# Half of modulation group 1 summed by TensorE with the pieces as weights, two first low parts ahead of the second sum, and later mLSTM numerators

## The chip, the cores and the metric

The kernel runs on one core of a Trainium2 chip. The metric is device time in microseconds (us) of one launch. TensorE (PE) does matrix products, VectorE (DVE) and ScalarE (ACT) elementwise work, GpSimd (POOL) masks and padding, and SyncE (SP) issues most of the transfers from the chip's memory.

## What is computed

Two transformer-like blocks follow each other on 256 positions of width 2048, batch 1, in float32. In both, a condition vector modulates the normalised input. Cut to what matters here:

```python
# first_block, for l in range(2)
c_act = silu(c)
mod = c_act @ ada_w[l] + ada_b[l]              # 2048 x 6144 weights
shift, scale, gate = split(mod, 3)
h = rms_norm(x, norm_g[l]) * (1.0 + scale) + shift
z = h @ w_in[l]
...
# second_block
mod = silu(c_2) @ w_ada_2[0] + b_ada_2[0]      # 2048 x 12288 weights, six parts
...
# bidirectional mLSTM, 4 heads of 256, d = forward, backward
num = sum over s of weight[t, s] * v[s]
den = sum over s of weight[t, s]
h_a = sum over d of num / max(|den|, exp(-m))
h_a = h_a * rsqrt(mean(h_a ** 2)) * g_head_a * sigmoid(oa)
mixed = concatenate([h_a, h_b]) @ w_out_2
```

## The kernel before

**Modulation.** The twelve parts (shift, scale, gate, ...) are twelve groups of 2048 columns. The 2048 rows of a group are read as 32 pieces (`AU`): in piece j each partition has 1024 values (`AC`) of one row, so that all of them are multiplied by one value of the condition, that of the partition in `c_act[:, 0, j]`. Partitions 0, 2, 4, ... carry one half of the columns and 1, 3, 5, ... the other (`CB2` is 2). DVE adds each piece, times its scalar, to an accumulator (`ada_start` for groups 0 and 1, `ada_add` for the others). When a group is complete, PE sums the accumulator over its partitions (`reduce_mod`): the accumulator's 128-column slices are the weights, and the moving operand has 128 columns, the last two of which are `halves_of`, one column for the even and one for the odd partitions. `mod_out` then adds the bias from PSUM into `mod`. Groups 0 and 1 (shift and scale of the first norm) must be complete before the first product of the kernel can start; groups 2 to 11 are added one piece per weight unit beside the products.

Groups 0 and 1 have an accumulator of twice the width (`ada_acc0`, `ada_acc1`), filled by turns, and a ring of eight slots (`FSLOTS`) of 512 KB, four in `ada_raw` and four in `ada_first`. SP (lines 549 to 552) issues the 64 pieces in order and, for each from the ninth on, first waits on `ada_used` until DVE has added the piece eight before. Behind them on SP's queue stand the units of the weight ring. From group 2 on the ring is the four slots of `ada_raw` (`ASLOTS`).

**Products.** Weights come in units of 512 KB (four 128-row tiles of 256 columns) into a ring of eight slots (`w_raw`). For most products ACT rounds a unit to its high part (`w_hi`, line 730), DVE subtracts (`w_lo`, line 1068), into rings of four slots (`PARTS`), and PE makes three matmuls per tile and half (high by high, low by high, high by low), all from line 1554. A block of 256 columns has four units over a contraction of 2048. Each engine walks the list `prods`; DVE and ACT prepare a block ahead (`ahead`, `prep`), and pieces of the modulation ride on the units (`ada_pieces`). The first product is `lat` of layer 0; its first four units are prepared by `prep(prods[0], 0, 0)`, which stands on DVE behind `mod_out(1)`.

**First norm.** `norm(0, ...)` on DVE computes `gainA` from `mod` group 1, then for each of 16 tiles the scaled tile (line 1108) and, two tiles later, its low part (line 1113); ACT makes the high part (line 773). With `by_tile`, the first block of `lat` takes the tiles one by one as they come ready.

**mLSTM.** It runs beside the product `out2b` (8 blocks of 2 units, 16 steps; nothing is split there), three steps to a head from step 3 on (`mlstm` on PE, ACT and DVE). In step 0 PE makes the head's scores into `bankS` and broadcasts the rows of direction 0 into `bankT`; in step 1 it broadcasts direction 1 and sums the squares of the head before (`head_sum`); in step 2 it makes, for each direction, the denominator into `stat` (`summed`) and the numerator into `bankO` (line 1828). `stat` and `bankO` each have one place: the second denominator waits until DVE has read the first (line 1430), the second numerator until DVE has read the first (line 1436). DVE's `head_output` divides both in step 0 of the next head. The last head's `head_output` and what follows it (`head_norm`, `head_low`) lead to `out2a`, a product with the mLSTM's output, 8 blocks of 2 units; PE's first block there waits unit by unit: the second unit needs all four heads.

Of the kernel before, what the change touches and what calls it, by code (L numbers as in the profile page):

```python
# [22 lines left out]
P = 128  # L23
T = 256
# [27 lines left out]
AC_T = AC // P  # L52
ASLOTS = 4
# [42 lines left out]
def program(nc, a, out):  # L96
# [3 lines left out]
    with ctx:  # L100
# [70 lines left out]
        c_raw = at("c_raw", W1 + 20, [P, 2, AU])  # L171
        W2 = W1 + 16 + CT * UW * 4 / 1024
# [72 lines left out]
        halves_done = sem("halves_done")  # L245
        const_loaded = sem("const_loaded")
# [187 lines left out]

        def by_half(x):

            return x.rearrange("p (c j) -> p c j", c=CB2)
# [110 lines left out]
        def _(sp):  # L548
# [129 lines left out]
        def _(act):  # L678
# [13 lines left out]
            act.activation(c_act[:], c_raw[:], ACT.Silu).then_inc(silu_done, 1)  # L692

# [324 lines left out]
        def _(dve):  # L1018
# [12 lines left out]
            def ada_add(n, j, m, fixed, rounds):  # L1031
# [3 lines left out]
                dve.wait_ge(ada_used, j + AU * n)  # L1035
# [4 lines left out]
            def mod_out(n):  # L1040

                stat_wait(dve, f"mod{n}")
                b = groups[n][2]
                ins = dve.tensor_tensor(by_half(mod[:, n, :]), summed_halves(stat), by_half(par[:, b:b + KT]), ALU.add)
                ins.then_inc(stat_read, 1)
                dve.wait_ge(stat_read, USE[f"mod{n}"] + 1)

            def ada_start(n):
                for j in range(AU):
                    slot, c = (AU * n + j) % FSLOTS, slice(j % 2 * AC, (j % 2 + 1) * AC)  # L1050
                    acc = acc_of(n)[:, c]
                    dve.wait_ge(ada_loaded[slot], 16 * ((AU * n + j) // FSLOTS + 1))
                    if n or j >= 2:
                        dve.wait_ge(ada_used, j + (AU * n - 1))
# [3 lines left out]
            def prep(g, i, k, before=None, beside=None, done=None):  # L1058


                for u, (k0, nk) in enumerate(g.units):
                    n, fixed = g.unit(i, k, u)
# [29 lines left out]
            def norm(r, buf, gain, scale, shift):  # L1092
# [13 lines left out]
                for t in range(KT + 2):  # L1106
                    if t < KT:
# [109 lines left out]
            ada_zero(2)  # L1217
            mod_out(1)
            prep(prods[0], 0, 0)
# [204 lines left out]
            def head_output(n):  # L1424
# [3 lines left out]
                link(dve.scalar_tensor_tensor(out=den[:, d, :], in0=stat[:, 0:T], scalar=-1.0, in1=floor_[:, d, :],  # L1428
                                              op0=ALU.mult, op1=ALU.max))
                dve.tensor_tensor(den[:, d, :], den[:, d, :], stat[:, 0:T], ALU.max).then_inc(stat_read, 1)  # L1430
# [5 lines left out]
                dve.tensor_tensor(dst, pairT(bankO[:]), inv, ALU.mult).then_inc(num_read, 1)  # L1436
# [82 lines left out]
        def _(pe):  # L1519
# [48 lines left out]
            def reduce_mod(n):  # L1568

                pe.wait_ge(ada_used, AU * (n + 1))  # L1570
# [16 lines left out]
            def norm(r):  # L1587
# [13 lines left out]
                if r in GAP_MOD:  # L1601
                    pe.wait_ge(ada_used, AU * (GAP_MOD[r] + 1))
# [72 lines left out]
            reduce_mod(0)  # L1675
            reduce_mod(1)
# [98 lines left out]

            def head_sum(h):
# [3 lines left out]
            def mlstm(_, s):  # L1780
# [22 lines left out]
                if step == 0:  # L1803
                    if h:
                        pe.wait_ge(wts_ready, 2 * h)
# [12 lines left out]
                else:  # L1818
                    for d in range(2):
                        n = 2 * h + d  # L1820
                        pe.wait_ge(wts_ready, n + 1)
                        summed(f"den{h}_{d}", [wts[:, d, t, :] for t in range(TT)])
                        if n:
                            pe.wait_ge(num_read, n)
                        for j in range(2):
                            for t in range(TT):
                                c = h * DHA + j * P
                                last = pe.matmul(bankO[:, j * T:(j + 1) * T], va_tok[:, t, c:c + P], wts[:, d, t, :],  # L1828
                                                 start=(t == 0), stop=(t == TT - 1))
                        last.then_inc(num_ready, 1)  # L1830
# [5 lines left out]
            multiply(G["out2a"], ready=(mix_ready, lambda t: 2 * LAYERS + t // 2))  # L1836
# [38 lines left out]
```

## Time and profile before

| | us |
|---|---|
| runs, median of 3 | 2349.02 |
| runs, lowest to highest | 2346.15 to 2352.45 |
| the profiled execution, its own time | 2352.27 |
| its span in the profile | 2350.4 |
| PE busy | 2213.0 |
| DVE busy | 1760.6 |
| ACT busy | 933.1 |

The profile is of one execution. Its span runs from the first to the last instruction recorded; its own time also holds what lies around them (1.9 us). Times of day in the rows are microseconds from the start of the span. A busy time is the time in which an engine had an instruction running; "idle before" is the time that it waited, with what released it.

### The profile page before, as it was taken

Reading aid. Unit: us, or ns where it says so; the run is one execution under the profiler, and the core shown is the slowest. Engines: PE = TensorE matmul, PEld = TensorE weight load, DVE = VectorE, ACT = ScalarE, POOL = GpSimd, SP = SyncE. Lnnn points to the kernel's source line nnn. Section 1 sums busy time; section 2 is a strip of 40 time slices with the busy share of each in tenths; the row PEclk is TensorE's granted clock in tenths of the full one; section 3 lists DMA queues with packets and bytes.
Section 4 is the critical chain, followed back from the end, with each engine's and each line's share of the span. In section 5 each row is a group of like instructions: output and inputs, shape, how many; then the busy total and the mean of one; then the engine's idle time right before and its main releaser. Section 6 shows DMA issues by size and latency. Waiting matters only on the chain.

```text
span 2350.4 us, 41402 instructions
## 1 busy us (share of the span) xinstructions
PE 2213.0 (94%) x16113; PEld 2108.5 (90%) x16113; DVE 1760.6 (75%) x2405; ACT 933.1 (40%) x1487; POOL 51.0 (2%) x63
## 2 busy tenths in 40 slices
PE   2399999999999999999999999889999999999998
PEld 2399997889999878899999987789999999999998
DVE  6899998797899977878868857778776665654444
ACT  2155405235543043354454422355544444433433
POOL 0000000000000000041000000000000000000000
PEclk9599999999999999999999999899999999999999
DMA  9989856895997487879949974267875655655553
GB/s 335 352 283 351 288 143 214 268 327 171 354 348 229 115 304 239 291 183 315 331 133 349 364 259 146 86 193 266 269 240 179 183 182 180 185 171 181 181 183 106
DMA packets 413240, 557.12 MB, mean 237 GB/s; under 512 B 25655, under 2 KB 362111, under 8 KB 412876
## 3 DMA queue, kind: packets, MB, share of 16 engines
q1 hardware_dynamic: 409536, 550.70, 71.1%
q0 software_dynamic: 1120, 2.18, 0.5%
q10 hardware_dynamic: 2476, 2.82, 0.3%
q8 instruction: 65, 1.06, 0.2%
q14 instruction: 43, 0.35, 0.0%
HBM read 553.47 MB, written 2.17 MB: 236 GB/s over the span
## 4 chain that ended last, share of the span: by engine, by line
PE 84%; DVE 6%; DMA 4%; issue 3%; ACT 2%; SPq 0%; POOL 0%; DVEq 0%; ACTq 0%; POOLq 0%
PE gemm L1554 79%; DMA ada_first<-in_ada_w 2%; DMA w_raw<-in_w_in 1%; DVE w_lo L1068 1%; PE stat L1576 1%; PE bankO L1631 1%; ACT w_hi L730 1%; DVE ada_odd L1036 1%; DVE ada_acc L1055 1%; DVE ada_even L1036 0%; PE bankS L1739 0%; PE bankS L1738 0%; DVE scr L1108 0%; PE bankO L1828 0%; DMA w_raw<-in_w_out 0%
## 5 line engine op out<-in xcount | busy, mean ns | idle before, releaser
L1068 DVE TENSOR_TENSOR w_lo<-w_raw,w_hi 128x1024 fp32r<-128x1024 f32 (+1 forms) x564 | 675.1, 1209 | 392.1 <-ACT w_hi L730 389.3
L1554 PE MATMUL gemm<-h_hi,w_hi 128*128 128x256 f32 (+2 forms) x3056 | 871.7, 285 | 23.8 <-DVE h_lo L1113 19.0
L1554 PE MATMUL gemm<-h_lo,w_hi 128*128 128x256 f32 (+2 forms) x3056 | 868.5, 284 | 0.0
L1554 PE MATMUL gemm<-h_hi,w_lo 128*128 128x256 f32 (+2 forms) x3056 | 868.3, 284 | 0.0
L730 ACT ACTIVATE w_hi<-w_raw 128x1024 fp32r<-128x1024 f32 (+1 forms) x564 | 571.7, 1028 | 642.6 <-PE gemm L1554 500.3
L1554 PEld LDWEIGHTS gemm<-h_hi,w_hi 128*128 128x128 f32 (+2 forms) x3056 | 587.6, 192 | 25.7 <-issue 21.6
L1554 PEld LDWEIGHTS gemm<-h_lo,w_hi 128*128 128x128 f32 (+2 forms) x3056 | 587.7, 192 | 0.5
L1554 PEld LDWEIGHTS gemm<-h_hi,w_lo 128*128 128x128 f32 (+2 forms) x3056 | 587.4, 192 | 0.3
L1036 DVE SCALAR_TENSOR_TENSOR ada_even<-ada_raw,c_act,ada_even 128x1024 f32<-128x1024 f32 x160 | 204.7, 1279 | 5.0 <-DMA ada_raw<-in_w_ada 2.0
L1554 PE MATMUL gemm<-G_hi,w_hi 128*128 128x256 f32 x704 | 199.3, 283 | 2.0 <-DVE G_lo L1508 2.0
L1554 PE MATMUL gemm<-G_hi,w_lo 128*128 128x256 f32 x704 | 199.2, 283 | 0.0
L1554 PE MATMUL gemm<-G_lo,w_hi 128*128 128x256 f32 x704 | 199.2, 283 | 0.0
L1263 DVE SCALAR_TENSOR_TENSOR conv<-u_pad,dwT,conv 128x256 f32<-128x256 f32 x480 | 192.5, 478 | 0.1
L1036 DVE SCALAR_TENSOR_TENSOR ada_odd<-ada_raw,c_act,ada_odd 128x1024 f32<-128x1024 f32 x128 | 163.7, 1279 | 6.0 <-DMA ada_raw<-in_ada_w 1.9
L1554 PEld LDWEIGHTS gemm<-G_hi,w_hi 128*128 128x128 f32 x704 | 135.2, 192 | 2.2 <-issue 2.2
L1554 PEld LDWEIGHTS gemm<-G_lo,w_hi 128*128 128x128 f32 x704 | 135.2, 192 | 0.0
L1554 PEld LDWEIGHTS gemm<-G_hi,w_lo 128*128 128x128 f32 x704 | 135.2, 192 | 0.0
L1554 PE MATMUL gemm<-mixsrc,w_raw 128*128 128x256 f32 x512 | 115.3, 380 | 1.6 <-ACT krT L717 1.6
L1554 PE MATMUL gemm<-h_full,w_raw 128*128 128x256 f32 x512 | 111.8, 379 | 0.0
L1554 PEld LDWEIGHTS gemm<-h_full,w_raw 128*128 128x128 f32 x512 | 97.1, 190 | 13.1
L1554 PEld LDWEIGHTS gemm<-mixsrc,w_raw 128*128 128x128 f32 x512 | 95.6, 190 | 14.3 <-ACT krT L717 2.2
L1554 PE MATMUL gemm<-m_hi,w_hi 128*128 128x256 f32 x256 | 73.1, 286 | 3.2 <-DVE m_lo L1153 3.2
(308 smaller groups left out, 2653.0 us busy)
## 6 DMA issues: line engine op xcount, KB each, us to landing
w_raw<-in_w_in SPq DMA_DIRECT2D x264, 512.0 KB, 5.5
w_raw<-in_w_up SPq DMA_DIRECT2D x176, 512.0 KB, 3.6
ada_raw<-in_ada_w SPq DMA_DIRECT2D x160, 512.0 KB, 7.1
ada_raw<-in_w_ada SPq DMA_DIRECT2D x160, 512.0 KB, 5.1
w_raw<-in_w_out SPq DMA_DIRECT2D x96, 512.0 KB, 6.5
w_raw<-in_w_down SPq DMA_DIRECT2D x64, 512.0 KB, 3.6
ada_first<-in_ada_w SPq DMA_DIRECT2D x32, 512.0 KB, 8.8
ada_late<-in_w_ada SPq DMA_DIRECT2D x32, 512.0 KB, 5.1
```

The lines of the kernel that those rows point to most:

```text
L730: act.activation(w_hi[:, fixed % PARTS, 0:sz], w_raw[:, fixed % RAW, 0:sz], ACT.Copy).then_inc(w_hi_done, 1)
L1036: dve.scalar_tensor_tensor(out=acc, in0=(ada_late if n == 11 else ada_raw)[:, slot, :], scalar=c_act[:, 0 if n < 6 else 1, bass.ds(m, 1)], ...
L1055: dve.scalar_tensor_tensor(out=acc, in0=first_slot(slot)[:, 0, :], scalar=c_act[:, 0, j:j + 1], in1=acc, op0=ALU.mult, op1=ALU.add).then_i ...
L1068: dve.tensor_tensor(w_lo[:, fixed % PARTS, 0:sz], w_raw[:, fixed % RAW, 0:sz], w_hi[:, fixed % PARTS, 0:sz].bitcast(F32), ALU.subtract).th ...
L1263: ins = dve.scalar_tensor_tensor(out=acc, in0=src, scalar=w, in1=acc, op0=ALU.mult, op1=ALU.add)
L1554: last = pe.matmul(half(g, k, q), left, right, start=(kt == 0 and j == 0), stop=(u == len(g.units) - 1 and t == nk - 1 and j == len(parts) ...
L1576: last = pe.matmul(stat[:, CB2 * t:CB2 * t + P], acc[:, j * AC + t * P:j * AC + (t + 1) * P], ones_and_halves[:, CB2:], start=(j == 0), st ...
L1631: last = pe.matmul(bankO[:, q0:T], v_of(h, kt), pt[:, n % 2, kt, q0:T], start=(kt == 0), stop=(kt == TT - 1))
```

## The change

It has four parts.

1. **Group 1.** The pieces with odd j of group 1 (16 of 32, `by_tensor`) are no longer added by DVE. PE takes each straight from its slot, as eight weights of 128 columns, against a moving operand of two columns: `c_pairs[:, j, :]`, the condition value times `halves_of`. ACT makes `c_pairs` with two small instructions after the silu, ahead of its transfers of the parameters. The result accumulates in `bankO`; `reduce_mod(1)` adds DVE's accumulator to the same place with 16 matmuls of two columns (before: 32 of 128 columns), and `mod_out(1)` reads `bankO`. SP waits on `pe_taken` for a slot that PE empties. The counts of `ada_used` shift (`added_before`).
2. **First low parts.** DVE's `prep` of the first four units is split: units 0 and 1 ahead of `mod_out(1)`, units 2 and 3 inside the first norm, before its tiles 4 and 8.
3. **mLSTM.** The numerator of direction 1 moves from step 2 to the start of step 0 of the next head (`head_num`). For the last head the second denominator goes to `bankT` and the second numerator to `bankS` (`apart`), with no wait on `stat` or `bankO`.
4. **`out2a`.** PE's first block goes by tile: tile t needs the heads up to its own.

```diff
+PE_PIECES = AU // 2
+        c_pairs = at("c_pairs", W1 + 20.25, [P, AU, CB2])
+        def apart(h, d):
+            return h == NHA - 1 and d == 1
+        def den_of(h, d):
+            return (bankT if apart(h, d) else stat)[:, 0:T]
+        def num_of(h, d):
+            return bankS if apart(h, d) else bankO
+        def by_tensor(n, j):
+            return n == 1 and j > 0 and j % 2 == 1
+        def added_before(n):
+            return AU * n - (PE_PIECES if n >= 2 else 0)
...
# SP
-                        sp.wait_ge(ada_used, j + (AU * m - ASLOTS + 1))
+                        if m == 2 and isinstance(j, int) and j < ASLOTS:
+                            sp.wait_ge(pe_taken, PE_PIECES)
+                        sp.wait_ge(ada_used, j + (added_before(m) - ASLOTS + 1))
...
-                    if n or j >= FSLOTS:
+                    if by_tensor(n, j - FSLOTS):
+                        sp.wait_ge(pe_taken, (j - FSLOTS) // 2 + 1)
+                    elif n and j >= FSLOTS:
+                        sp.wait_ge(ada_used, AU + (j - FSLOTS) // 2 + 1)
+                    elif n or j >= FSLOTS:
                         sp.wait_ge(ada_used, AU * n + j - FSLOTS + 1)
                     ada_load_first(n, j)
# ACT, after the silu
+            act.wait_ge(silu_done, 1)
+            act.wait_ge(halves_done, 1)
+            for c in range(CB2):
+                ins = act.activation(c_pairs[:, :, c], c_act[:, 0, :], ACT.Copy, scale=halves_of[:, c:c + 1])
+            ins.then_inc(c_paired, 1)
# DVE
             def ada_start(n):
-                for j in range(AU):
-                    slot, c = (AU * n + j) % FSLOTS, slice(j % 2 * AC, (j % 2 + 1) * AC)
+                own = [j for j in range(AU) if not by_tensor(n, j)]
+                for i, j in enumerate(own):
+                    slot, c = (AU * n + j) % FSLOTS, slice(i % 2 * AC, (i % 2 + 1) * AC)
...
                 for t in range(KT + 2):
+                    if r == 0 and t in (4, 8):
+                        prep(prods[0], 0, 0, us=(t // 4 + 1,))
...
             mod_out(0)
             ada_zero(2)
+            prep(prods[0], 0, 0, us=(0, 1))
             mod_out(1)
-            prep(prods[0], 0, 0)
# PE
             def reduce_mod(n):
+                if n == 1:
+                    for t in range(AC_T):
+                        for j in range(n_acc):
+                            last = pe.matmul(bankO[:, CB2 * t:CB2 * (t + 1)], acc[:, j * AC + t * P:j * AC + (t + 1) * P],
+                                             halves_of, start=False, stop=(t == AC_T - 1 and j == n_acc - 1))
+                    last.then_inc(stat_ready, 1)
+                    return
...
             reduce_mod(0)
+            pe.wait_ge(c_paired, 1)
+            pe.wait_ge(tr_read, PAR_TR + 1)
+            for j in range(1, AU, 2):
+                slot = (AU + j) % FSLOTS
+                pe.wait_ge(ada_loaded[slot], 16 * ((AU + j) // FSLOTS + 1))
+                for t in range(AC_T):
+                    last = pe.matmul(bankO[:, CB2 * t:CB2 * (t + 1)], first_slot(slot)[:, 0, t * P:(t + 1) * P],
+                                     c_pairs[:, j, :], start=(j == 1 and t == 0), stop=False)
+                last.then_inc(pe_taken, 1)
             reduce_mod(1)
...
+            def head_num(h, d):
+                n = 2 * h + d
+                if n and not apart(h, d):
+                    pe.wait_ge(num_read, n)
+                for j in range(2):
+                    for t in range(TT):
+                        c = h * DHA + j * P
+                        last = pe.matmul(num_of(h, d)[:, j * T:(j + 1) * T], va_tok[:, t, c:c + P], wts[:, d, t, :],
+                                         start=(t == 0), stop=(t == TT - 1))
+                last.then_inc(num_ready, 1)
...
                 if step == 0:
                     if h:
+                        head_num(h - 1, 1)
                         pe.wait_ge(wts_ready, 2 * h)
...
                     for d in range(2):
-                        n = 2 * h + d
-                        pe.wait_ge(wts_ready, n + 1)
-                        summed(f"den{h}_{d}", [wts[:, d, t, :] for t in range(TT)])
-                        if n:
-                            pe.wait_ge(num_read, n)
-                        for j in range(2):
-                            for t in range(TT):
-                                c = h * DHA + j * P
-                                last = pe.matmul(bankO[:, j * T:(j + 1) * T], va_tok[:, t, c:c + P], wts[:, d, t, :],
-                                                 start=(t == 0), stop=(t == TT - 1))
-                        last.then_inc(num_ready, 1)
+                        pe.wait_ge(wts_ready, 2 * h + d + 1)
+                        if not apart(h, d):
+                            stat_write(pe, f"den{h}_{d}")
+                        for t in range(TT):
+                            last = pe.matmul(den_of(h, d), ones[:], wts[:, d, t, :], start=(t == 0), stop=(t == TT - 1))
+                        last.then_inc(stat_ready, 1)
+                        if d == 0 or apart(h, d):
+                            head_num(h, d)
...
-            multiply(G["out2a"], ready=(mix_ready, lambda t: 2 * LAYERS + t // 2))
+            multiply(G["out2a"], ready=(mix_ready, lambda t: 2 * LAYERS + (t + 1) // 2), by_tile=True)
```

## Rows read from the trace of the kernel before

**Rows 1.** The profile's page: span, busy time by engine, shares of the chain that ended last.

```profile
span 2350.4 us, 41402 instructions
...
PE 2213.0 (94%) x16113; PEld 2108.5 (90%) x16113; DVE 1760.6 (75%) x2405; ACT 933.1 (40%) x1487; POOL 51.0 (2%) x63
...
PE 84%; DVE 6%; DMA 4%; issue 3%; ACT 2%; SPq 0%; POOL 0%; DVEq 0%; ACTq 0%; POOLq 0%
```

**Rows 2.** Waits of PE, whole span: who <- for whom: total, times, longest (us).

```profile
PE stat L1576 <- DVE mod L1044: 38.0, 1, 38.0
...
PE stat L1565 <- DVE den L1430: 5.3, 2, 4.8
...
PE bankO L1828 <- DVE hA L1436: 3.8, 4, 1.3
```

**Rows 3.** Timeline of DVE, 106 to 123 us: start, length, line, instruction, [idle before].

```profile
105.76 3.67 DVE L1055 SCALAR_TENSOR_TENSOR ada_acc<-ada_first,c_act,ada_acc 128x1024 f32<-128x1024 f32 x3
...
116.02 0.17 DVE L1044 TENSOR_TENSOR mod<-stat,par 128x16 f32<-128x16 f32 x1 [5.32 <-PE stat L1576]
116.23 4.63 DVE L1068 TENSOR_TENSOR w_lo<-w_raw,w_hi 128x1024 fp32r<-128x1024 f32 x4
```

**Rows 4.** Stretches: busy PE, PEld, DVE, ACT, POOL; then PE clock, DMA share, GB/s.

```profile
74.00:76.00 2.00, 0.00 (x0) 0.00 (x0) 2.00 (x3) 0.00 (x0) 0.00 (x0) 0.50 0.83 281
102.00:104.00 2.00, 0.00 (x0) 0.00 (x0) 2.00 (x3) 0.00 (x0) 0.00 (x0) 0.50 1.03 412
130.00:140.00 10.00, 10.00 (x86) 10.00 (x85) 9.66 (x16) 8.95 (x17) 0.00 (x0) 1.00 0.35 104
```

**Rows 5.** Pieces issued from line 552 that land after 107 us, window 100 to 108.

```profile
L552 SPq DMA_DIRECT2D ada_first<-in_ada_w x1: 535/535/535, 99.9 to 99.9; - x1
...
DMA to landing us min/median/max: 7.8/7.8/7.8
```

**Rows 6.** Timeline of ACT, first weight units, 100 to 123 us.

```profile
110.69 1.06 ACT L730 ACTIVATE w_hi<-w_raw 128x1024 fp32r<-128x1024 f32 x1 [0.45 <-DMA w_raw<-in_w_in]
```

**Rows 7.** Timeline of PE, the first 130 us.

```profile
58.44 7.03 PE L1671 MATMUL bankT<-ident,dw_rows 31*128 31x31 f32 x32
...
109.66 6.25 PE L1576 MATMUL stat<-ones_and_halves,ada_acc 128*128 128x128 f32 x32 [38.04 <-DVE mod L1044]
122.80 0.55 PE L1554 MATMUL gemm<-h_hi,w_hi 128*128 128x256 f32 x1 [6.88 <-DVE h_lo L1113]
```

**Rows 8.** Timelines behind the first norm: SP, DVE, ACT, DVE, 128 to 172 us.

```profile
128.29 0.38 SPq L571 DMA_DIRECT2D w_raw<-in_w_in  x1
...
134.08 1.23 DVE L1068 TENSOR_TENSOR w_lo<-w_raw,w_hi 128x1024 fp32r<-128x1024 f32 x1 [0.34 <-ACT w_hi L730]
...
168.25 1.06 ACT L730 ACTIVATE w_hi<-w_raw 128x1024 fp32r<-128x1024 f32 x1 [2.36 <-DMA w_raw<-in_w_in]
...
170.56 1.22 DVE L1068 TENSOR_TENSOR w_lo<-w_raw,w_hi 128x1024 fp32r<-128x1024 f32 x1
```

**Rows 9.** Timeline of PE, mLSTM and the start of out2a, 1410 to 1512 us.

```profile
1420.32 1.99 PE L1828 MATMUL bankO<-wts,va_tok 128*128 128x256 f32 x8 [1.32 <-DVE hA L1436]
...
1490.51 2.04 PE L1565 MATMUL stat<-wts,ones_and_halves 128*128 128x256 f32 x4 [4.81 <-DVE den L1430]
1492.93 3.78 PE L1828 MATMUL bankO<-wts,va_tok 128*128 128x256 f32 x8 [0.38 <-DVE hA L1436]
...
1508.48 0.58 PE L1554 MATMUL gemm<-hA_hi,w_hi 128*128 128x256 f32 x1 [4.30 <-DVE hA_lo L1153]
```

**Rows 10.** Timeline of DVE, after the first head, and from the last head to out2a.

```profile
1428.65 0.69 DVE L1414 TENSOR_TENSOR decay<-bankT,lower 128x512 f32<-128x512 f32 x1 [4.24 <-PE bankT L1814]
...
1496.82 0.69 DVE L1436 TENSOR_TENSOR htmp<-bankO,den 128x512 f32<-128x512 f32 x1 [1.24 <-PE bankO L1828]
...
1507.66 0.69 DVE L1153 TENSOR_TENSOR hA_lo<-hA,hA_hi 128x512 fp32r<-128x512 f32 x1 [0.70 <-ACT hA_hi L809]
...
1509.34 2.29 DVE L1068 TENSOR_TENSOR w_lo<-w_raw,w_hi 128x1024 fp32r<-128x1024 f32 x2
```

More of the change, by code:

```diff
@@ L245, in program @@
         halves_done = sem("halves_done")
+        c_paired = sem("c_paired")
+        pe_taken = sem("pe_taken")
         const_loaded = sem("const_loaded")
@@ L1034, in ada_add @@
                 dve.wait_ge(ada_loaded[slot], rounds * 16)
-                dve.wait_ge(ada_used, j + AU * n)
+                dve.wait_ge(ada_used, j + added_before(n))
                 dve.scalar_tensor_tensor(out=acc, in0=(ada_late if n == 11 else ada_raw)[:, slot, :],
@@ L1043, in mod_out @@
                 b = groups[n][2]
-                ins = dve.tensor_tensor(by_half(mod[:, n, :]), summed_halves(stat), by_half(par[:, b:b + KT]), ALU.add)
+                total = bankO[:, 0:KT].rearrange("p (j c) -> p c j", c=CB2) if n == 1 else summed_halves(stat)
+                ins = dve.tensor_tensor(by_half(mod[:, n, :]), total, by_half(par[:, b:b + KT]), ALU.add)
                 ins.then_inc(stat_read, 1)
@@ L1048, in ada_start, with prep @@
             def ada_start(n):
-                for j in range(AU):
-                    slot, c = (AU * n + j) % FSLOTS, slice(j % 2 * AC, (j % 2 + 1) * AC)
+                own = [j for j in range(AU) if not by_tensor(n, j)]
+                for i, j in enumerate(own):
+                    slot, c = (AU * n + j) % FSLOTS, slice(i % 2 * AC, (i % 2 + 1) * AC)
                     acc = acc_of(n)[:, c]
                     dve.wait_ge(ada_loaded[slot], 16 * ((AU * n + j) // FSLOTS + 1))
-                    if n or j >= 2:
-                        dve.wait_ge(ada_used, j + (AU * n - 1))
+                    if n or i >= 2:
+                        dve.wait_ge(ada_used, i + (AU * n - 1))
                     dve.scalar_tensor_tensor(out=acc, in0=first_slot(slot)[:, 0, :], scalar=c_act[:, 0, j:j + 1],
                                              in1=acc, op0=ALU.mult, op1=ALU.add).then_inc(ada_used, 1)
-            def prep(g, i, k, before=None, beside=None, done=None):
+            def prep(g, i, k, before=None, beside=None, done=None, us=None):
                 for u, (k0, nk) in enumerate(g.units):
+                    if us is not None and u not in us:
+                        continue
                     n, fixed = g.unit(i, k, u)
@@ L1427, in head_output @@
                 stat_wait(dve, f"den{h}_{d}")
-                link(dve.scalar_tensor_tensor(out=den[:, d, :], in0=stat[:, 0:T], scalar=-1.0, in1=floor_[:, d, :],
+                total = den_of(h, d)
+                link(dve.scalar_tensor_tensor(out=den[:, d, :], in0=total, scalar=-1.0, in1=floor_[:, d, :],
                                               op0=ALU.mult, op1=ALU.max))
-                dve.tensor_tensor(den[:, d, :], den[:, d, :], stat[:, 0:T], ALU.max).then_inc(stat_read, 1)
+                dve.tensor_tensor(den[:, d, :], den[:, d, :], total, ALU.max).then_inc(stat_read, 1)
                 dve.wait_ge(stat_read, USE[f"den{h}_{d}"] + 1)
@@ L1435, in head_output @@
                 dst = hA[:, 2 * h:2 * h + 2, :] if d == 0 else htmp[:]
-                dve.tensor_tensor(dst, pairT(bankO[:]), inv, ALU.mult).then_inc(num_read, 1)
+                dve.tensor_tensor(dst, pairT(num_of(h, d)[:]), inv, ALU.mult).then_inc(num_read, 1)
                 dve.wait_ge(num_read, n + 1)
@@ L1568, in reduce_mod @@
             def reduce_mod(n):
-                pe.wait_ge(ada_used, AU * (n + 1))
+                pe.wait_ge(ada_used, added_before(n + 1))
                 stat_write(pe, f"mod{n}")
@@ L1601, in norm @@
                 if r in GAP_MOD:
-                    pe.wait_ge(ada_used, AU * (GAP_MOD[r] + 1))
+                    pe.wait_ge(ada_used, added_before(GAP_MOD[r] + 1))
                     mod_tiles(reversed(range(GAP_FIRST, AC_T)))
```

## The prediction

> **What bounds the kernel now.** I read the page first: PE is busy for 2213.0 of 2350.4 us and holds 84% of the chain that ended last [rows 1]. So a change pays where PE stands still, or stands at the lower clock, and nowhere else. The waits of PE then say where that is: one of 38.0 us, for `mod_out(0)` ahead of the second sum of the modulation, two of 5.3 us together for a denominator to be read, four of 3.8 us for a numerator's place [rows 2], and 4.30 us for the last low part ahead of `out2a` [rows 9]. The change aims at each of these. The timeline, the stretches and the landings then tell what would end last once the named wait is gone.
>
> **Part 1, group 1.** DVE adds 32 pieces at one per 1.2 us (three in 3.67 us) and ends at 109.4 [rows 3]. PE sums from 109.66 to 115.9 [rows 7], `mod_out(1)` runs at 116.02, four low parts take 4.6 us [rows 3], and the first product starts at 122.80 [rows 7]. Halving DVE's pieces would save 16 x 1.2 = 19 us if DVE alone were the bound. It isn't: the DMA engines have a busy share of 1.03 and move 412 GB/s at 102 to 104 us [rows 4]. A piece of 524,288 bytes takes 1.27 us of that, more than DVE's 1.2. The last piece, issued at 99.9, lands 7.8 us later, at 107.7, so DVE was hardly behind it [rows 5]. What a faster emptying of slots can win is the ramp at the start: at 74 to 76 us only 281 GB/s moved [rows 4], because eight slots were full and DVE freed one per 1.2 us. PE and DVE together free almost two in that time. Over the 8 us of ramp some 0.8 MB more can move: 0.8 MB / 412 GB/s = 1.9 us, bounded by 0 (nothing gained on the ramp) and 3 us (no ramp at all). I take 1.7: the last piece lands at 106.0.
>
> The kernel before shows no matmul with two columns. Bounds: the parameter transposes have 31 columns at the lower clock and go at 7.03/32 = 0.22 us each [rows 7]; with half the time at the upper clock it is 0.11; and a matmul that overlaps nothing took 0.55 [rows 7]. I take 0.215, as the nearest row has few moving columns too and 128 weights. A piece is 8 of them, 1.7 us; TensorE gets one piece per two landings, 2.55 us, so it keeps up, 16 x 1.7 = 27 us within 34. After the last landing come 1.7 us for that piece and 16 x 0.215 = 3.4 us for `reduce_mod(1)` (before, 32 in 6.25 us [rows 7]); with 0.3 us of handovers `mod_out(1)` runs at 111.4 instead of 116.02. Few rows bear on the clock here: I count on the lower one, 1.2 GHz.
>
> The Trainium skill, "DMA: Bandwidth & Descriptors", section Where 436 GB/s comes from, says that for loads from memory the limit per core is about 358 GB/s. The trace disagrees, with 412 GB/s [rows 4]. By the page 24 pieces would take 35 us from the first landing and the estimate for the last one would be 111 us, some 5 us later than mine; the case before already had it at 107.7.
>
> **Part 2, first low parts.** Units 0 and 1 are split while PE sums. The second unit's high part started at 110.69, on its landing [rows 6]; the landings stand behind the pieces on one queue, so they move up by the same 1.7 us, to 109.0. High part 1.06, low part 1.2: ready at 111.3, level with `mod_out(1)`. So all 4.6 us leave the path there, and 2.4 us come back inside the norm, which DVE runs without a gap. From `mod_out(1)` to the first product is now 6.78 us, less 4.63: the first product starts at 111.4 + 2.2 = 113.6, 9.2 us sooner. The norm on DVE then ends 2.4 us later after that start. The second block's first low part was ready at 134.08 + 1.23 = 135.3 [rows 8], 12.5 after the start. PE needed it when its first block ended: unit 0 was used by 128.29 [rows 8], and 72 matmuls at 0.12 (86 in 10 us [rows 4]) end at 136.9, 14.1 after the start. With 2.4 more it is ready at 14.9: a new stall of 0.8 us. Beyond it the transfers restart later against PE. Unit 19 landed for ACT at 168.25, and its low part began at 170.56 [rows 8], ended at 171.8, and PE needed it at 174.3 (136.9, 11 units of 24 x 0.12 = 2.88 and the 4 narrow ones of half): slack 1.2 + 2.5 = 3.7 us, more than 2.4. I cost that at nothing; if the cover is gone it is up to 2 us. Front of the kernel: 9.2 - 0.8 = **8.4 us**, bounds 5.5 (no ramp gained, 2 us of stall) and 10.
>
> ACT's two small instructions ahead of the parameters delay their issue by some 0.6 us. What hides it is the stream of group 0's pieces, which takes until long after; without the cover PE would start the odd pieces 0.6 us later, with eight already loaded: nothing. SP's new waits queue the first units behind the last pieces as before.
>
> **Part 3, mLSTM.** The second numerator waits for the first to be read: 1.32 us in the first head [rows 9], 3.8 - 0.4 = 3.4 us in three heads [rows 2], some 4 us measured from the last start to the next, since the ends of matmuls overlap. Moved behind 16 matmuls of the product (3.5 us), it finds the place free. DVE's second division then comes some 1.2 us later, in a stretch where DVE stands idle for 4.24 us [rows 10]. Gain **3.9 us**, bounds 2.5 and 4.
>
> In the last head PE stands for 4.81 us, then makes both matmul groups at the lower clock (8 in 3.78 us, against 1.99 in the first head) [rows 9]. But this isn't the path: DVE runs on from there to the last low part at 1507.66, and in all of it waits for PE only 1.24 us [rows 10]. With `bankT` and `bankS` the numerator is there by 1490. So 1.2 us go, not 8.
>
> **Part 4, `out2a`.** At 1508.48 PE had 24 matmuls left of its first block [rows 9], at 0.21 us (1.2 GHz): end 1513.6. By tile it does 12 of them ahead of the last head. The remaining 12 end 1.4 (2.4 GHz) to 2.6 us after a start 1.2 us sooner: 1508.7 to 1509.8. DVE has the next block's first low part at 1510.5 [rows 10] less 1.2 = 1509.3, so no great stall. Gain from 1513.6 to 1509.8: **3.8 us** (the 1.2 is in it), bounds 2 and 4.5. The order by tile in the second pass of the loop changes no count.
>
> **Sum.** 8.4 + 3.9 + 3.8 = 16.1 us, against the profiled execution's own 2352.3: 2336.2. That execution was 3.3 us above the median of the runs, so the time to expect is 2349.0 - 16.1, rounded to **2333**. Everything else is PE-bound and just comes sooner.
>
> **Rivals.** *Two-column matmuls don't overlap (slower).* Place: PE, 72 to 110 us. If each of 144 costs what a lone one does, 0.55 us, the sum ends at 72 + 79 = 151; `mod_out(1)` then at 151.2. The front loses when `mod_out(1)` passes 119.8 and the whole when it passes 127.5, that is from (127.5 - 72)/144 = 0.385 us each. At 0.55: 31 - 8 = 23 us slower, 2372. For it: no row has two columns, and each loads its own weights. Against: 0.22 with 31 columns. Chance 0.03.
>
> *The transfers aren't the bound.* Then PE's 27 us end at 99, `mod_out(1)` is at 103, and the front gives 16 us: 2325. Against: the share of 1.03 for 20 us. 0.05.
>
> *The first blocks give it back.* PE enters the stretch of products where the transfers are full with 2.4 us less of a lead, the stall of 0.8 us grows to 3 and no ramp is gained: the front gives 4.5 us: 2337. For it: ACT stood for a weight unit for 2.36 us at 168 us [rows 8]. 0.15.
>
> *Pieces land at 1.46 us each once many are under way.* The last lands at 111, `mod_out(1)` follows at 116.4, the front gives 3.4: 2338. Against: 1.27 us measured with six under way [rows 4, 5]. 0.02. It is what the 358 GB/s of the Trainium skill, cited above, would make of it.
>
> *The mLSTM gives little.* If numerators in step 0 delay the scores, DVE and ACT end last: 4 instead of 7.7 us, 2337. Against: DVE's idle time there. 0.10.
>
> *The change doesn't act on the end:* DVE's chain stays and the clock falls in the new gap, about 3.8 us, ahead of the squares' sum; its price, 12 matmuls at 0.21, is in the bounds.
>
> My forecast has 0.65: its own range is 2329 to 2337. The range that should hold the time reaches to the third, fourth and fifth: **2327 to 2340**, with about 2 us of scatter of the medians in it. A measurement of this kernel can tell 0.3%, 7 us, from no change. Faster by more: 0.94; within: 0.03; slower: 0.03.
>
> **What would show it.** In the profile after: 16 pieces on line 1055 for group 1, DVE idle on landings between them at a DMA share above 1; two-column matmuls in runs of eight of 1.7 us; `mod_out(1)` near 111.4 and the first product near 113.6; a wait of about 0.8 us for `w_lo` some 14 us behind that; no wait at the numerators; PE's last wait for a low part near 1495 on the new scale, with 12 matmuls behind it. A first product later than 117, or DVE's low parts late against PE from 140 to 260 us, makes the forecast wrong.

## The result and the profile after

| | before | after |
|---|---|---|
| median | 2349.69 | 2354.30 |
| lowest to highest of 20 runs | 2346.15 to 2353.07 | 2349.56 to 2360.51 |
| the profiled execution, its own time (span) | 2352.27 (2350.4) | 2353.44 (2351.6) |

The ratio is 1.0018, with a 95% interval of 1.0011 to 1.0025: 4.6 us slower by the medians, within 0.3%. The forecast was 2333. The two profiled executions lie closer together, 1.2 us in their spans: that of before ran 2.6 us above its median, that of after 0.9 below.

The page of the kernel after, against [rows 1]:

```profile
span 2351.6 us, 41890 instructions
...
PE 2259.3 (96%) x16369; PEld 2155.9 (92%) x16369; DVE 1743.6 (74%) x2389; ACT 934.6 (40%) x1489; POOL 51.0 (2%) x63
...
PE 83%; DVE 6%; DMA 5%; ACT 3%; issue 1%; ACTq 1%; SPq 0%; POOL 0%; DVEq 0%; POOLq 0%
```

The counts say it at once. DVE has 16 instructions fewer, as planned. PE has 256 more. The diff adds 16 pieces of 8 matmuls, which is 128. The second sum stays as it was, 16 matmuls in the source (8 slices of two halves) and x32 in the trace, before and after; the account of the change above set the 32 of the trace beside the 16 of the source, as if the sum were halved. So 128 matmuls of source are 256 instructions: a matmul of float32 operands is one call in the source and two instructions of the trace. Not every matmul is: the five transposes of line 1664 are five rows in the trace of before, and the first product, whose operands are rounded parts (`fp32r`), has one row per call, 96 for its first block.

PE's timeline of the kernel after, 60 to 130 us (an x32 here is two pieces, or the second sum):

```profile
65.35 5.34 PE L1625 MATMUL stat<-ones_and_halves,ada_acc 128*128 128x128 f32 x32
70.53 3.63 PE L1731 MATMUL bankO<-c_pairs,ada_raw 128*128 128x2 f32 x32
74.02 5.76 PE L1731 MATMUL bankO<-c_pairs,ada_first 128*128 128x2 f32 x32
79.64 6.97 PE L1731 MATMUL bankO<-c_pairs,ada_raw 128*128 128x2 f32 x32
...
113.77 6.96 PE L1731 MATMUL bankO<-c_pairs,ada_first 128*128 128x2 f32 x32
120.60 6.97 PE L1619 MATMUL bankO<-ones_and_halves,ada_acc 128*128 128x2 f32 x32
129.84 0.55 PE L1596 MATMUL gemm<-h_hi,w_hi 128*128 128x256 f32 x1 [2.28 <-DVE h_lo L1154]
```

From one start to the next, the first two pieces took 3.49 us, 0.109 per instruction; from 79.64 on it is 6.83 us, 0.213 each, and no row has a wait. So a piece takes 3.41 us where two pieces can land per 2.55 us, and the sum behind them 6.97 us. The last piece starts at about 117.2. Its weights had long landed: SP could issue the transfer only at 107.1, when PE had emptied the slot, but it was there 4.3 us later, at 111.4 (before: issued at 99.9, there at 107.7 [rows 5]).

Stretches of the kernel after: busy PE, PEld, DVE, ACT, POOL with counts; then granted PE clock, DMA share, GB/s.

```profile
70.00:74.00 4.00, 4.00 (x39) 4.00 (x38) 3.96 (x4) 0.00 (x0) 0.00 (x0) 1.00 0.15 28
76.00:80.00 4.00, 4.00 (x20) 4.00 (x21) 1.60 (x3) 0.00 (x0) 0.00 (x0) 0.50 0.99 363
90.00:100.00 10.00, 10.00 (x49) 10.00 (x48) 4.76 (x4) 0.00 (x0) 0.00 (x0) 0.50 0.94 319
112.00:130.00 18.00, 15.72 (x74) 15.66 (x75) 4.78 (x9) 5.54 (x7) 0.00 (x0) 0.50 0.80 264
```

The granted clock was 1.00 (2.4 GHz) at 70 to 74 us, behind the 128-column matmuls of the first sum. It fell to 0.50 (1.2 GHz) once only two-column matmuls were running and stayed there for 50 us, though PE was busy for all of 90 to 100. In that stretch 319 GB/s moved, against 412 in [rows 4]: the slots wait for PE, and two pieces per 3.41 us are 307 GB/s. DVE, at 4.76 of 10 us, waits for pieces.

DVE's timeline of the kernel after, against [rows 3]:

```profile
105.64 1.28 DVE L1092 SCALAR_TENSOR_TENSOR ada_acc<-ada_first,c_act,ada_acc 128x1024 f32<-128x1024 f32 x1 [1.99 <-DMA ada_first<-in_ada_w]
109.00 1.28 DVE L1092 SCALAR_TENSOR_TENSOR ada_acc<-ada_first,c_act,ada_acc 128x1024 f32<-128x1024 f32 x1 [2.07 <-DMA ada_first<-in_ada_w]
...
114.81 1.23 DVE L1107 TENSOR_TENSOR w_lo<-w_raw,w_hi 128x1024 fp32r<-128x1024 f32 x1 [3.25 <-ACT w_hi L765]
116.27 1.23 DVE L1107 TENSOR_TENSOR w_lo<-w_raw,w_hi 128x1024 fp32r<-128x1024 f32 x1 [0.23 <-ACT w_hi L765]
127.60 0.17 DVE L1080 TENSOR_TENSOR mod<-bankO,par 128x16 f32<-128x16 f32 x1 [10.11 <-PE bankO L1619]
...
130.40 1.22 DVE L1107 TENSOR_TENSOR w_lo<-w_raw,w_hi 128x1024 fp32r<-128x1024 f32 x1
```

DVE ended its last piece at 110.3 and both first low parts at 117.5, then stood for 10.11 us. `mod_out(1)` runs at 127.60 instead of 116.02, the first product at 129.84 instead of 122.80: 7.0 us later, where the forecast had it 9.2 sooner.

The rest of the kernel can be followed by one kind of instruction that every version has at the same places, DVE's reciprocals. Start in each version less start before, in us (worked out from the timelines):

| start before | place | after | e1 | e2 | e3 | e4 | e5 | e6 | e7 |
|---|---|---|---|---|---|---|---|---|---|
| 400.63 | first layer | +9.4 | -1.8 | +1.5 | -2.9 | -0.7 | -1.3 | -3.2 | -4.9 |
| 1186.52 | second block | +8.5 | -3.2 | +1.6 | -4.5 | -3.3 | -4.0 | -2.9 | -7.2 |
| 1417.79 | first mLSTM head | +8.7 | -4.8 | 0.0 | -6.1 | -1.0 | -2.3 | -6.8 | -5.6 |
| 1490.39 | last head | +4.9 | -8.9 | -4.1 | -10.3 | -5.2 | -6.1 | -11.0 | -9.7 |
| 1557.96 | behind `out2a` | +1.2 | -13.5 | -8.7 | -13.8 | -8.8 | -9.4 | -14.4 | -14.3 |
| 2334.96 | end | +1.2 | -12.0 | -7.2 | -12.3 | -7.3 | -7.9 | -12.9 | -14.3 |

So the front lost 9.4 us, the heads gave 3.8 back (8.7 to 4.9) and the last head with `out2a` 3.7 (4.9 to 1.2). Between norms single profiles move by a microsecond or two either way (e4, whose front is that of before, is at -0.7 and -3.3). One such step can be read: ahead of the first mLSTM head every profile has some us at the lower clock, and e1 has fewer of them than before (at 1404 to 1409 us the granted clock was 0.56 before and 1.00 in e1, with 13 and 21 matmuls). The rest isn't explained, and no verdict below rests on it.

The profile's timelines of PE and DVE of the kernel after, mLSTM's last two heads and `out2a`:

```profile
1492.21 1.13 PE L1894 MATMUL bankT<-wts,ones_and_halves 128*128 128x256 f32 x4 [1.60 <-DVE wts L1462]
...
1512.12 0.40 PE L1596 MATMUL gemm<-hA_hi,w_hi 128*128 128x256 f32 x1 [2.68 <-DVE hA_lo L1194]
```

```profile
1475.47 0.69 DVE L1478 TENSOR_TENSOR htmp<-bankO,den 128x512 f32<-128x512 f32 x1 [1.75 <-PE bankO L1841]
...
1500.53 0.69 DVE L1478 TENSOR_TENSOR htmp<-bankS,den 128x512 f32<-128x512 f32 x1
...
1511.37 0.69 DVE L1194 TENSOR_TENSOR hA_lo<-hA,hA_hi 128x512 fp32r<-128x512 f32 x1 [0.70 <-ACT hA_hi L844]
```

The waits of [rows 9] and [rows 10] have gone: 4.81 us for the denominator, the 1.32 for a numerator's place, and DVE's 1.24 for the last numerator. What takes their place is DVE's wait of 1.75 us for the moved numerator of the head before, in a stretch where it has time. PE's wait for the last low part is 2.68 instead of 4.30. The gap that the forecast named ahead of the squares' sum is there too: PE stands 4.14 us for them, and DVE, which makes the path there, doesn't wait for it.

### The profile page after: what moved, and what is told of

Same layout as the page of the kernel before. It is cut to its first block, busy times and chain, and to the rows that moved or that the text cites. A ratio compares the mean times of both kernels' runs of the same rounds, so it can differ in the third digit from the quotient of the medians.

```text
span 2351.6 us, 41890 instructions
## 1 busy us (share of the span) xinstructions
PE 2259.3 (96%) x16369; PEld 2155.9 (92%) x16369; DVE 1743.6 (74%) x2389; ACT 934.6 (40%) x1489; POOL 51.0 (2%) x63
## 4 chain that ended last, share of the span: by engine, by line
PE 83%; DVE 6%; DMA 5%; ACT 3%; issue 1%; ACTq 1%; SPq 0%; POOL 0%; DVEq 0%; POOLq 0%
PE gemm L1596 76%; DMA w_raw<-in_w_in 2%; PE bankO L1731 2%; DMA pos_i<-in_positions 1%; DVE w_lo L1107 1%; ACT w_hi L765 1%; DVE ada_odd L1071 1%; DMA w_raw<-in_w_out 1%; PE stat L1625 1%; PE bankO L1680 1%; DVE ada_even L1071 1%; ACTq L738 1%; DVE scr L1149 1%; ACTq L733 0%; PE bankS L1797 0%
```

## The experiments

The theory after the result: part 1 alone is at fault, because TensorE executes twice the instructions that I counted, at the lower clock, and so becomes the bound. The rivals: the first low parts or the later parts cost something; a TensorE piece costs more than its instructions (waits, slots); it is the clock and not the count; the transfers hold back what is left. The letters in the quoted texts are those of the theories as each text words them. Every version was timed beside the kernel before, and its ratio is to that. The kernel before had a median of 2350.93 us beside e1 to e4, 2350.38 beside e5 to e7 and 2349.69 beside the kernel after, so a difference between medians of different groups is good to about a microsecond.

**e1: all but part 1.** The kernel before with the parts 2, 3 and 4.

```diff
+            prep(prods[0], 0, 0, us=(0, 1))
             mod_out(1)
-            prep(prods[0], 0, 0)
```

> Parts 2, 3 and 4 without part 1: DVE adds all 32 pieces of group 1 and the sum goes with 128 columns, as before. Theory A (TensorE's share of group 1 is what costs: a float32 matmul is two instructions, so a piece is 16 x 0.215 us at 1.2 GHz): the second sum ends at 115.9 as before, the first product starts near 118.5, and with the mLSTM's 7.5 us the kernel takes 2349.7 - 2.5 - 7.5 = 2340 us. Rival B (the low parts inside the norm and the later restart of the transfers cost, not the sum): the front stays above the kernel before, the total at 2345 or more.

Measured: 2340.56 us, ratio 0.9956 (0.9943 to 0.9968). Part 1 by itself makes the kernel 13.7 us slower by the medians, 13.2 by the table's last row, 14.6 by the ratios (1.0018 and 0.9956). PE and then DVE in the timelines of e1:

```profile
110.61 5.44 PE L1593 MATMUL stat<-ones_and_halves,ada_acc 128*128 128x128 f32 x32 [39.02 <-DVE mod L1056]
118.32 0.36 PE L1571 MATMUL gemm<-h_hi,w_hi 128*128 128x256 f32 x1 [2.28 <-DVE h_lo L1129]
...
120.95 0.38 PE L1571 MATMUL gemm<-h_hi,w_hi 128*128 128x256 f32 x1 [0.95 <-DVE h_lo L1129]
...
125.25 0.38 PE L1571 MATMUL gemm<-h_hi,w_hi 128*128 128x256 f32 x1 [0.95 <-DVE h_lo L1129]
...
223.30 0.39 PE L1571 MATMUL gemm<-h_hi,w_hi 128*128 128x256 f32 x1 [0.77 <-DVE w_lo L1082]
```

```profile
111.69 2.36 DVE L1082 TENSOR_TENSOR w_lo<-w_raw,w_hi 128x1024 fp32r<-128x1024 f32 x2
116.08 0.17 DVE L1056 TENSOR_TENSOR mod<-stat,par 128x16 f32<-128x16 f32 x1 [2.04 <-PE stat L1593]
```

With the sum where it was, `mod_out(1)` is where it was (116.08) and both low parts are hidden. The first product starts 4.48 us sooner. Part of this goes again: the low parts inside the norm make PE wait for the next tile twice, 0.95 us each, and a low part is 0.77 us late at 223 us. What it comes to is seen from PE's own starts (each matmul of the products against the same one before): 4.5 us sooner at the first, 3.7 at the end of the first block, 2.6 behind the wait at 223 us. The two waits of 1.9 us cost less than 1, because e1's first block ran at the upper clock from its start (granted 1.00 at 120 to 130 us, 0.58 before, where a matmul came each 0.21 us until 128). It couldn't use all of that: DVE needs 0.79 us for a tile of the norm, six matmuls at 0.12 only 0.72, so that the block, 14.1 us long before, took 14.8. The table's -1.8 at 400 us lies behind the next norm, where another 0.8 us goes that isn't explained. So part 2 pays, but about half of what it takes off the path.

**e2: every fourth piece.** TensorE takes 8 of the 32 pieces.

```diff
-            return n == 1 and j > 0 and j % 2 == 1
+            return n == 1 and j > 0 and j % 4 == 3
```

> The whole change, but TensorE takes every fourth piece of group 1 (8) instead of every second (16). Theory A: 8 x 3.4 = 27 us are less than the 33 us of landings, so the last piece is taken 3.4 us after it lands near 106, the sum's 32 instructions take 7 us, mod_out(1) comes near 116.6 instead of 127.6, and the kernel takes about 2340 us. Rival C (slots that TensorE empties hold up the one queue of transfers): landings stay late, near 114, and the total stays within 4 us of the changed kernel's 2354.

Measured: 2345.16 us, ratio 0.9974 (0.9965 to 0.9984); 9.1 us below the kernel after, but 5 above what I expected. PE's timeline of e2:

```profile
103.36 3.58 PE L1731 MATMUL bankO<-c_pairs,ada_raw 128*128 128x2 f32 x16 [2.73 <-DMA ada_raw<-in_ada_w]
108.53 3.58 PE L1731 MATMUL bankO<-c_pairs,ada_first 128*128 128x2 f32 x16 [1.60 <-DMA ada_first<-in_ada_w]
111.97 6.96 PE L1619 MATMUL bankO<-ones_and_halves,ada_acc 128*128 128x2 f32 x32
121.21 0.55 PE L1596 MATMUL gemm<-h_hi,w_hi 128*128 128x256 f32 x1 [2.28 <-DVE h_lo L1154]
```

A piece is 16 instructions and 3.58 us here, one at a time. With half as many, PE waits for each (1.60, 2.73) and is no longer the bound. The expectation missed by the last landing: it had `mod_out(1)` at 116.6 and it ran at 118.97, since the last piece was taken on its landing at 108.5 and not near 106. The forecast's ramp term had gone into this expectation too. That is 2.4 of the 5 us. Behind it the first product starts 1.6 us sooner than before, and the table has +1.5 at 400 us: the blocks give back more than was expected.

**e3: 128 moving columns.** The same weights, the pair of columns repeated 64 times, into `bankO` and `bankS`, in the second sum of group 1 too; `mod_out(1)` reads two columns of each slice.

```diff
-                    last = pe.matmul(bankO[:, CB2 * t:CB2 * (t + 1)], first_slot(slot)[:, 0, t * P:(t + 1) * P],
-                                     c_pairs[:, j, :], start=(j == 1 and t == 0), stop=False)
+                    last = pe.matmul(wide_of(t), first_slot(slot)[:, 0, t * P:(t + 1) * P],
+                                     c_pairs[:, j, :].unsqueeze(1).to_broadcast([P, P // CB2, CB2]),
+                                     start=(j == 1 and t % 4 == 0), stop=False)
```

> The whole change, but each of TensorE's matmuls in group 1 has 128 moving columns (the pair 64 times over, into two banks) instead of 2; same weights, same count. Theory A with the clock: instructions of 128 columns go at 0.2 us too at 1.2 GHz, so nothing is lost; if the granted clock rises to 2.4 GHz they go at 0.11, a piece takes 1.8 us, landings set the pace, mod_out(1) comes near 111.5 and the kernel takes about 2336 us. If the clock stays at 1.2 GHz the time is the changed kernel's, 2354. Rival D (the columns have no part in the clock; TensorE is held at 1.2 GHz by what else runs there): 2354, granted clock 0.5.

Measured: 2338.40 us, ratio 0.9947 (0.9933 to 0.9961), 15.9 us below the kernel after with the same count of instructions. Stretches of e3, columns as above:

```profile
70.00:74.00 4.00, 4.00 (x32) 4.00 (x32) 3.96 (x4) 0.00 (x0) 0.00 (x0) 0.84 0.11 27
74.00:76.00 2.00, 2.00 (x20) 2.00 (x19) 2.00 (x2) 0.00 (x0) 0.00 (x0) 1.00 0.84 270
76.00:80.00 4.00, 3.77 (x34) 3.58 (x34) 1.44 (x2) 0.00 (x0) 0.00 (x0) 1.00 0.93 323
90.00:100.00 10.00, 8.01 (x64) 7.44 (x64) 4.90 (x5) 0.00 (x0) 0.00 (x0) 1.00 1.03 411
```

Timelines of e3, first PE, then DVE:

```profile
108.48 1.16 PE L1741 MATMUL bankO<-c_pairs,ada_first 128*128 128x128 f32 x8 [0.61 <-DMA ada_first<-in_ada_w]
109.48 1.05 PE L1741 MATMUL bankS<-c_pairs,ada_first 128*128 128x128 f32 x8
110.37 1.95 PE L1628 MATMUL bankO<-ones_and_halves,ada_acc 128*128 128x128 f32 x16
112.16 1.95 PE L1628 MATMUL bankS<-ones_and_halves,ada_acc 128*128 128x128 f32 x16
116.55 0.36 PE L1605 MATMUL gemm<-h_hi,w_hi 128*128 128x256 f32 x1 [2.44 <-DVE h_lo L1163]
```

```profile
114.15 0.17 DVE L1085 TENSOR_TENSOR mod<-bankO,par 128x8 f32<-128x8 f32 x1 [0.37 <-PE bankS L1628]
```

The clock stays at 1.00 through 90 to 100 us with PE busy for 8.01 of 10, where in the kernel after it is 0.50 with 10.00 of 10. That excludes rival D. From one start to the next an instruction takes 1.79/16 = 0.112 us (110.37 to 112.16), a piece 1.9 us, and the transfers are the bound again at 411 GB/s, with a wait for each piece. Sixty-four times the columns, then, in half the time. The time was 2.4 us above the 2336 expected: `mod_out(1)` ran at 114.15 and not near 111.5, again because the last piece landed at 108.5 and not at 106.0. Against e1, where DVE adds the whole group, this is only 1.9 us sooner (116.08 to 114.15), and the totals, 2338.40 and 2340.56, have intervals that overlap. So part 1, without its fault, brings the second sum forward by 1.9 us, and in the total these runs can't tell it from nothing.

**e4: the end alone.** The kernel before with the parts 3 and 4, no change in front.

```diff
-            multiply(G["out2a"], ready=(mix_ready, lambda t: 2 * LAYERS + t // 2))
+            multiply(G["out2a"], ready=(mix_ready, lambda t: 2 * LAYERS + (t + 1) // 2), by_tile=True)
```

> The kernel before with parts 3 and 4 alone (later numerators, out2a by tile). Both theories: the front is that of before; heads give 3.9 us and the last head with out2a 3.7, so 2349.7 - 7.5 = 2342 us. If the mLSTM gives less alone than in the changed kernel, 2346 or more.

Measured: 2343.64 us, ratio 0.9965 (0.9954 to 0.9977). In the table the heads give 4.2 us (-1.0 to -5.2) and the last head with `out2a` 3.6 (-5.2 to -8.8). Against e1 part 2 is worth 3.1 us by the medians, with intervals that overlap, and 1.1 in the table's first row. Over all versions of the table the heads give 3.8 to 4.2 us and the last head with `out2a` 3.3 to 4.6.

**e5: half the slices.** TensorE takes only every second 128-column slice of its pieces, so a piece is 8 instructions. This leaves half of those pieces out of the modulation of group 1.

```diff
-                for t in range(AC_T):
+                for t in range(0, AC_T, 2):
```

> The changed kernel, but TensorE takes only every second 128-column slice of its 16 pieces (the other half of the columns stays without the odd rows, so the output differs): 8 instructions of two columns per piece, as the forecast counted them, instead of 16. Theory A (count times 0.215 us at 1.2 GHz): a piece takes 1.75 us, less than the 2.55 us of two landings; the last is taken near 110, the sum's 32 instructions end near 117, mod_out(1) near 117.3 instead of 127.6, the kernel near 2345 us. Rival C (TensorE's slots hold up the queue of transfers, whatever a piece costs): mod_out(1) stays later than 123 and the kernel above 2350.

Measured: 2341.31 us, ratio 0.9961 (0.9949 to 0.9974). PE's timeline of e5:

```profile
105.80 1.87 PE L1731 MATMUL bankO<-c_pairs,ada_first 128*128 128x2 f32 x8 [0.69 <-DMA ada_first<-in_ada_w]
108.38 1.86 PE L1731 MATMUL bankO<-c_pairs,ada_first 128*128 128x2 f32 x8 [0.71 <-DMA ada_first<-in_ada_w]
110.10 6.96 PE L1619 MATMUL bankO<-ones_and_halves,ada_acc 128*128 128x2 f32 x32
119.34 0.55 PE L1596 MATMUL gemm<-h_hi,w_hi 128*128 128x256 f32 x1 [2.28 <-DVE h_lo L1154]
```

And a stretch of e5, columns as above:

```profile
90.00:100.00 10.00, 6.89 (x31) 6.54 (x30) 5.14 (x4) 0.00 (x0) 0.00 (x0) 0.50 1.03 409
```

This is the piece that the forecast had, 8 instructions at 0.215 us, at the lower clock still. It fits between two landings with 0.7 us to spare, and 13 us of the loss are gone. `mod_out(1)` ran at 117.11, as expected (117.3); the kernel was 3.7 us faster than the 2345 expected by its median, while its profiled execution took 2344.28. The transfers run at 409 GB/s here, so rival C is excluded. So the lower clock alone didn't do it, nor did anything that a TensorE piece has beside its instructions: all waits, slots and releases are those of the kernel after. The count and the clock do it together, and either one put right is enough.

**e6: wide, and DVE's sum in one half.** e3, with DVE's 16 pieces of group 1 added into one half of the accumulator, so that the second sum has half the instructions.

```diff
-                    slot, c = (AU * n + j) % FSLOTS, slice(i % 2 * AC, (i % 2 + 1) * AC)
+                    slot, c = (AU * n + j) % FSLOTS, slice(i % 2 * AC, (i % 2 + 1) * AC) if n == 0 else slice(0, AC)
```

> 128 moving columns, and DVE's 16 pieces all in one half of its accumulator, so that the second sum has 16 instructions instead of 32. DVE waits for landings anyway, so its longer chain costs nothing. If the end of the second sum sets the front: mod_out(1) 1.8 us sooner, 112.4, and the kernel 2336.6 us. If the transfers behind it set the pace from 130 to 240 us (theory E): mod_out(1) is sooner by that much too, but less than 1 us of it is left at 400 us, and the kernel takes 2338.

Measured: 2337.56 us, ratio 0.9945 (0.9932 to 0.9958), the fastest version that computes the whole result, though not to be told from e3. Its PE and DVE:

```profile
109.01 1.16 PE L1743 MATMUL bankO<-c_pairs,ada_first 128*128 128x128 f32 x8 [1.68 <-DMA ada_first<-in_ada_w]
...
111.80 1.05 PE L1630 MATMUL bankS<-ones_and_halves,ada_acc 128*128 128x128 f32 x8
117.14 0.55 PE L1607 MATMUL gemm<-h_hi,w_hi 128*128 128x256 f32 x1 [4.28 <-DVE h_lo L1165]
```

```profile
113.09 1.22 DVE L1118 TENSOR_TENSOR w_lo<-w_raw,w_hi 128x1024 fp32r<-128x1024 f32 x1 [0.20 <-ACT w_hi L769]
114.23 0.16 DVE L1085 TENSOR_TENSOR mod<-bankO,par 128x8 f32<-128x8 f32 x1
```

The second sum ended at 112.9, 1.2 us sooner than in e3, and nothing came of it: `mod_out(1)` now stands behind the low part of unit 1, which ends at 114.2 and hangs on that unit's landing. The expectation (112.4) missed this. The first product starts even 0.6 us later than in e3. The transfers of this run landed some 0.5 us later (the last piece was taken at 109.0, not 108.5), ACT's high parts followed them, and the norm's first high part with it (115.98, not 115.39). And PE, idle for 4.28 us instead of 2.44, came back at the lower clock (granted 0.50 at 116 to 120 us, 1.00 in e3). With PE cured, the order of DVE's queue and the landings are next.

**e7: wide, half of group 2's bytes.** e3 with only half of each piece of group 2 transferred. This leaves half of the columns of group 2 of the modulation out, and takes 8 MB off the transfers beside the first products.

```diff
+                if n == 2:
+                    sp.dma_start(ada_raw[:, slot:slot + 1, 0:AC // 2], src[:, :, :, 0:AC // 2]).then_inc(ada_loaded[slot], 16)
+                    return
```

> 128 moving columns, and of each piece of group 2 (which rides on the first products) only half is transferred; the rest of its slot holds old values, so the output differs. DVE's and TensorE's work is the same. Theory E (the transfers of the first products keep back what the front gains: first product 6.3 us sooner, only 2.9 left at 217 us): ACT's waits for units between 128 and 262 us fall from 51 us to under 15, the wait of TensorE near 230 us for a low part goes, and 1 to 2 us more are left: 2337 us. If DVE's two low parts inside the norm are all that is given back, nothing changes: 2338.4 and the same wait.

Measured: 2338.21 us, ratio 0.9946 (0.9934 to 0.9959). PE's waits of e3, 112 to 265 us (total, times, longest), then those of e7 in the same stretch:

```profile
PE gemm L1605 <- DVE h_lo L1163: 4.3, 3, 2.4
PE gemm L1605 <- DVE w_lo L1116: 1.5, 2, 1.2
```

```profile
PE gemm L1608 <- DVE h_lo L1166: 3.0, 2, 2.4
```

ACT's waits for the transfer of a unit, 128 to 262 us, fell from 51.4 us to 1.8. The late low parts, 0.30 us at 172 and 1.20 at 223, are gone with the bytes, and the table has e7 2.0 us ahead of e3 at 400 us. By PE's starts all of this comes at those two places. The 1.3 us less of waits for `h_lo` gain nothing: e7's PE ran its first matmuls at a lower clock (0.63 at 116 to 120 us), so it waited less for DVE, and both end the first block at 131.4 us. So the transfers do hold back the blocks behind the first norm, by some 2 us. Whether that lasts isn't shown: at 1418 us e7 is 0.5 us behind e3, at the end 2.0 ahead, and by the medians 0.2, less than the intervals can tell.

## Why the forecast was wrong, point by point

- **What bounds the kernel**, right: e1, e3 and e4 gain where PE stood before.
- **Part 1, the price of a piece**, wrong, and the step that failed: "A piece is 8 of them, 1.7 us", "16 x 0.215 = 3.4 us for `reduce_mod(1)`". The duration was right (0.213), the count was half. [Rows 7] had it: 16 matmuls of source stand there as x32, both for the second sum (8 slices of two halves) and in line 1671, the row that the 0.22 us was read from. The forecast set 16 for the sum after beside "before, 32 in 6.25 us", and so counted source against trace. A piece is 16 instructions and 3.41 us, the sum 32 and 6.97. "It keeps up" turned into PE being the bound by 3.41 against 2.55, and `mod_out(1)` came at 127.60 instead of 111.4. e5 shows it by restoring the count, e1 by leaving part 1 out.
- **The clock**, as forecast, but with a consequence not seen: it was set down as a price per matmul, and never asked whether the change itself made it so. The kernel after stays at 1.2 GHz, e3 at 2.4. The Trainium skill, "TensorE: Matmul & The Clock Gate", section LDWEIGHTS (loading the stationary operand), gives a weight load of P columns as about P/1.2 ns, which for 128 makes an estimate of 107 ns. That is near the spacing of instructions at the upper clock, 0.109 us with 2 moving columns (from 70.53) and 0.112 with 128 (e3), and half of the 0.213 at the lower one; that section doesn't say for which clock it holds. It is the spacing that compares: a single weight load is recorded as 0.19 us at the upper clock and 0.33 at the lower, and they overlap.
- **Part 1, the ramp**, wrong: worth 0 instead of 1.7 us. The last piece was taken at 108.4 to 109.0 in e2, e3, e5 and e6. [Rows 4] had this too: at 74 to 76 us the DMA share was 0.83 already, and in e3 it is 0.93 at 76 to 80 for 323 GB/s. The engines were mostly busy there, and free slots could add little; e3, with slots emptied sooner, took its last piece no sooner than before. This term is missing from part 1 even where the count is put right: e3's `mod_out(1)` at 114.15 is 1.9 us ahead of before, where the forecast had 4.6.
- **Part 2**: the low parts left the path as forecast (e1: 4.48 of 4.63 us). The way back was put at 0.8 us, as a stall at the second block, and at nothing beyond. In e1 the second block stalls for 0.1; the two waits of 0.95 us come in the first block itself, where I had let DVE run on without asking which tile PE was at, and cost 0.8 net; and the wait of 0.77 at 223 us is the term put at nothing. By PE's starts 1.9 of the 4.5 us are gone there. Part 2 is worth 2.6 us then, 1.8 at 400 us and 3.1 by the medians, where the forecast had 3.8. In the kernel after the same places cost 0.79 and 1.24. The way back lies between my own 0.8 and the 3 us of the rival of the first blocks giving it back.
- **Parts 3 and 4**, right: 3.9 forecast and 3.8 measured (4.2 in e4), 3.8 and 3.7 (3.6). The second has its two terms as well: DVE's reciprocals gain 1.2 us within the last head, its wait for the numerator, and 2.5 from there to behind `out2a`. The moved numerator comes to DVE 1.75 us late, not 1.2, in idle time as forecast.
- **The rivals.** The slower one had the place and the engine right: two-column matmuls on PE. It had the mechanism wrong, since they overlap well. Its break-even, 0.385 us per matmul of source, was passed by 2 x 0.213 = 0.43. By its own sum of 144 that is 72 + 62 = 134; the first pieces ran at the upper clock and `mod_out(1)` came at 127.6, the very point given, 127.5, from which the whole loses. It lost 1.2 us in the profiled span, 4.6 by the medians. The chance of 0.03 was read off a duration alone; a doubt about the count would have belonged there.
- **The sum.** With the measured terms: front +9.4, heads -3.8, the rest of the mLSTM and `out2a` -3.7, together +1.9, and +1.2 in the spans; the steps between are the small shifts left open above.

## What to carry to other kernels

Take the number of instructions for an added operation from a row of the trace that has its operand types, and check it against the source: here each float32 matmul was two. When an engine gets work so as to relieve another, compare its time per piece at the lower clock with the time between landings. Try wide moving operands where the weights cost the same anyway: here 128 columns in place of two took the kernel from 0.18% slower to 0.5% faster. Ask also what is left to gain where transfers set the pace: with its fault cured, the half of group 1 on TensorE brought `mod_out(1)` 1.9 us forward. A place that is free on one engine's queue isn't free for the engine that consumes tile by tile behind it.

## What the runs showed of the hardware that I had not expected

- PE, busy for all of 76 to 112 us with two-column matmuls, was granted a clock of 0.50, and so it was in e5, busy for 6.89 of 10; with 128 columns and a busy time of 8.01 of 10 us it was granted 1.00. Before the fall it had run 128-column matmuls.
- An instruction with 128 columns of weights came each 0.109 us with 2 moving columns and each 0.112 with 128, both at the upper clock; each 0.213 with 2 at the lower.
- A matmul of float32 operands was two instructions in the trace; a transpose, and a matmul of the rounded parts (`fp32r`), was one.
